# Where a weight tile is split around three norms in a two-layer diffusion trunk: ahead of the modulation instead of behind it

## What is computed

```python
def rmsnorm(x, g):
    y = xf * lax.rsqrt(jnp.mean(xf * xf, axis=-1, keepdims=True) + EPS)
    return (y * g.astype(jnp.float32)).astype(x.dtype)
def modulate(x, shift, scale):
    return x * (1 + scale) + shift
...
for layer in range(DEPTH):
    hp = modulate(rmsnorm(xp, norm1_g[layer]), p_sh1, p_sc1)
    hs = modulate(rmsnorm(xs, norm1_g[layer]), s_sh1, s_sc1)
    # layer 0: Hyena convolution and mLSTM; layer 1: windowed attention -> yp, ys
    xp = xp + p_g1 * yp
    xs = xs + s_g1 * ys
    hp = modulate(rmsnorm(xp, norm2_g[layer]), p_sh2, p_sc2)
    hs = modulate(rmsnorm(xs, norm2_g[layer]), s_sh2, s_sc2)
    # layer 0: dense SwiGLU (1024 -> 2816 -> 1024); layer 1: two of eight expert SwiGLUs
    xp = xp + p_g2 * fp
    xs = xs + s_g2 * fs
```

## Time and profile before

| what | value |
|---|---|
| three runs | 1495.99, 1496.56, 1505.28 us; median 1496.56 |
| profiled execution | 1495.99 us |
| its span in the trace | 1494.2 us, 16385 instructions |
| PE busy | 1365.6 us, 91% |
| DVE busy | 1044.5 us, 70% |
| ACT busy | 818.6 us, 55% |
| weight splits, ACT L494 (raw and arena) | 326 casts, 1.90 us each |
| weight splits, DVE L501 (raw and arena) | 326 subtractions, 2.28 us each |
| mean granted clock of PE | 0.955 of full |

### The profile page before, as it was taken

The page is one execution under the profiler, slowest core; times in us unless marked ns, Lnnn a source line. Parts: engine busy times, 40 slices in busy tenths (PEclk is TensorE's granted clock), DMA queues, the critical chain, the costliest instruction groups (busy, mean ns, idle before and its releaser), DMA issues.

```text
span 1494.2 us, 16385 instructions
## 1 busy us (share of the span) xinstructions
PE 1365.6 (91%) x6400; PEld 1067.1 (71%) x6400; DVE 1044.5 (70%) x1015; ACT 818.6 (55%) x908; POOL 25.4 (2%) x44
## 2 busy tenths in 40 slices
PE   5888898589999987788999999999999999999994
PEld 1555463268888766777888888888888888888783
DVE  0473336455554476556889889898898998988985
ACT  1433121144334455445777777777777777777772
POOL 3000000000000020000000000000000000000000
PEclk9899998699999999888999999999999999999997
DMA  9888677255566540244999999999999999999990
GB/s 330 285 284 307 232 252 264 90 167 170 172 194 188 179 129 32 86 169 141 339 365 351 356 334 353 365 357 352 332 347 364 364 350 341 347 349 369 351 348 30
DMA packets 288116, 400.94 MB, mean 268 GB/s; under 512 B 15973, under 2 KB 224064, under 8 KB 287968
## 3 DMA queue, kind: packets, MB, share of 16 engines
q1 hardware_dynamic: 282048, 391.23, 77.2%
q0 software_dynamic: 1792, 4.28, 1.0%
q10 hardware_dynamic: 4192, 4.31, 0.8%
HBM read 397.93 MB, written 1.84 MB: 268 GB/s over the span
## 4 chain that ended last, share of the span: by engine, by line
PE 79%; DVE 4%; ACT 2%; DMA 1%; issue 1%; SPq 0%; DVEq 0%; ACTq 0%
PE bank L1740 76%; PE bank L2097 2%; DMA raw<-in_w_ada 1%; PE bank L1791 1%; ACT arena L1027 1%; PE bank L2196 0%; ACT arena L1037 0%; SPq L602 0%; DVE arena L1730 0%; DVE xn L1179 0%; DVE arena L1504 0%; DVE x L1505 0%; DVE x L1731 0%; DVE Gb L1198 0%; ACT Gb L796 0%
## 5 line engine op out<-in xcount | busy, mean ns | idle before, releaser
L501 DVE TENSOR_TENSOR w_lo<-raw,w_hi 128x2048 fp32r<-128x2048 f32 (+1 forms) x238 | 543.3, 2283 | 154.4 <-ACT w_hi L494 153.1
L494 ACT CAST w_hi<-raw 128x2048 fp32r<-128x2048 f32 (+1 forms) x238 | 451.8, 1898 | 165.4 <-PE bank L1740 94.2
L1740 PE MATMUL bank<-w_hi,x_hi 128*128 128x512 f32 x1072 | 436.2, 407 | 23.1 <-issue 15.3
L1740 PE MATMUL bank<-w_lo,x_hi 128*128 128x512 f32 x1072 | 424.9, 396 | 0.0
L1740 PE MATMUL bank<-w_hi,x_lo 128*128 128x512 f32 x1072 | 422.4, 394 | 0.0
L1740 PEld LDWEIGHTS bank<-w_hi,x_hi 128*128 128x128 f32 x1072 | 203.5, 190 | 71.6 <-issue 26.3
L1740 PEld LDWEIGHTS bank<-w_hi,x_lo 128*128 128x128 f32 x1072 | 203.7, 190 | 47.0
L1740 PEld LDWEIGHTS bank<-w_lo,x_hi 128*128 128x128 f32 x1072 | 204.1, 190 | 39.2 <-issue 0.2
L501 DVE TENSOR_TENSOR w_lo<-arena,w_hi 128x2048 fp32r<-128x2048 f32 x88 | 201.7, 2292 | 36.9 <-ACT w_hi L494 36.9
L494 ACT CAST w_hi<-arena 128x2048 fp32r<-128x2048 f32 x88 | 168.0, 1909 | 27.8 <-PE bank L1740 27.8
L1740 PE MATMUL bank<-w_hi,g_hi 128*128 128x512 f32 x440 | 174.0, 395 | 1.8 <-DVE g_lo L1461 1.8
(11 more groups left out here) (285 smaller groups left out, 940.6 us busy)
## 6 DMA issues: line engine op xcount, KB each, us to landing
raw<-in_moe_w SPq DMA_DIRECT2D x352, 512.0 KB, 5.4
arena<-in_moe_w SPq DMA_DIRECT2D x176, 512.0 KB, 5.4
raw<-in_w_ada SPq DMA_DIRECT2D x96, 512.0 KB, 6.7
raw<-in_ff_w SPq DMA_DIRECT2D x66, 512.0 KB, 4.5
raw<-in_ev_w_in SPq DMA_DIRECT2D x28, 512.0 KB, 6.8
raw<-in_at_w_qkv SPq DMA_DIRECT2D x12, 512.0 KB, 4.6
raw<-in_ev_w_out SPq DMA_DIRECT2D x8, 512.0 KB, 7.7
raw<-in_at_w_out SPq DMA_DIRECT2D x8, 512.0 KB, 4.6
```

Source lines behind the costliest of these rows:

```text
L494: nc.scalar.copy(w_hi[:, t % SPL, c], place[:, c]).then_inc(hi_ok, 1)
L501: nc.vector.tensor_tensor(w_lo[:, t % SPL, c], raw_slot(n)[0][:, c], w_hi[:, t % SPL, c].bitcast(F32), ALU.subtract).then_inc(lo_ok, 1)
L1740: return pe.matmul(out, lhsT, rhs, start=start, stop=stop)
```

## The change

On ACT the three `high` calls of norms 1, 2 and 3 move from behind `take_turned` to in front of it, and so does one `low` call of each seam on DVE. At norm 2 it is the low part of QKV0 + 1 that moves on DVE, while on ACT it is the high part of QKV0 + 2; the low part of QKV0 + 2 stays. No instruction is added or left out, and the streams of PE, SP and POOL stay as they are.

```diff
@@ -967,8 +967,8 @@
             norm_root(1)
+            high(FF0 + 2)
             take_turned(2, 2)
-            high(FF0 + 2)
             for c in range(NCH):
@@ -980,8 +980,8 @@
             eng.wait_ge(stored_st, STATE_STORES)
             norm_root(2)
+            high(QKV0 + 2)
             take_turned(3, 1)
-            high(QKV0 + 2)
             def take_qkv(w):
@@ -1042,8 +1042,8 @@
             eng.wait_ge(stored_kv, 32)
             norm_root(3)
+            high(MOE0 + 2)
             take_turned(5, 3)
-            high(MOE0 + 2)
             warm(ACT.Exp)
@@ -1487,8 +1487,8 @@
             norm_rows(1)
+            low(FF0 + 2)
             take_turned(2, 2)
-            low(FF0 + 2)
             gate_source(1)
@@ -1508,8 +1508,8 @@
             norm_rows(2)
+            low(QKV0 + 1)
             take_turned(3, 1)
-            low(QKV0 + 1)
             low(QKV0 + 2)
@@ -1613,8 +1613,8 @@
             norm_rows(3)
+            low(MOE0 + 2)
             take_turned(5, 3)
-            low(MOE0 + 2)
             L, E = rw[:, 0:16].rearrange("p (g e) -> p g e", g=G), rw[:, 16:32].rearrange("p (g e) -> p g e", g=G)
```

## The result

The changed kernel took 1512.05 us (median of 22 runs, 1501.18 to 1522.61), the kernel before 1497.69 us (22 runs beside them, 1493.90 to 1510.11): ratio 1.0076, 95% interval 1.0056 to 1.0095. That is within 1% of no change, but outside the range I gave (1498.0 to 1506.5). The profiled execution took 1515.6 us (span 1513.8), 19.6 us more span than the profiled one of before. Over all 39 executions recorded of the changed kernel (these 22 among them) the time goes with the mean granted clock: 12 took 1501 to 1507 us at 0.951 to 0.955, 27 took 1510 to 1523 us at 0.941 to 0.947.

The account below looks back on a forecast made before the run. The prediction took PE to bound the kernel, with time to win or lose only at the three norm seams. Later starts of 4.0 us plus 2.35 of clock made 6.3 us, so 1502.6 us, range 1498.0 to 1506.5.

Parts of the forecast that it names:

- The starts: At the three norm seams, PE's next work starts later by 2.0, 0.3 and 1.7 us, 4.0 us in all.
- DVE's order decides: First seam: DVE's modulation waits for the moved subtraction, so PE's first wide matmul starts 1.99 us later.
- POOL beside the subtraction: Second seam: POOL's memset adds 0 to the moved DVE subtraction; upper bound 0.9 us.
- The clock at the first seam: Behind the first seam: one half-speed stretch of PE follows the longer gap, +1.65 us, bounds 0 to 3.3.
- The clock at the router: Third seam: all the router's first matmuls run at the half level, +0.7 us, bounds 0 and 0.9.
- the stretch from there to the end of the experts otherwise of the same length: Sign to check: after the first seam's half level, no other change in length through the experts, attention included.
- B: Rival: first and second seams each get a second half-speed stretch, 9.6 us in all, 1505.9 us; chance 0.13.
- C: Rival: not slower; second seam's restart and router both run at the full level, giving back 3.95 us, 1496.3; chance 0.05.
- A: Rival: later starts alone, first seam again escapes the half level, +4.0 us, about 1500.3; chance 0.22.

Follow-up runs that it names:

- highs-only run: Kernel before with only ScalarE's three high splits moved ahead of the turned rows, VectorE's low splits left behind them: 1499.50 us, ratio 1.0015.
- run with pauses: Kernel before with no split moved; VectorE does idle work on a free buffer where the change has its splits: 1511.76 us, ratio 1.0082.
- norm 3 alone: Kernel before with both splits of norm 3 only moved, as in the change: 1501.34 us, ratio 1.0014.
- norm 1 alone: Kernel before with both splits of norm 1 only moved, as in the change: 1500.24 us, ratio 1.0008.
- norm 2 alone: Kernel before with both splits of norm 2 only moved, as in the change: 1501.02 us, ratio 1.0014.
- attention filled: Kernel before with matmuls of constants filling PE's gaps in the attention stage only, no split moved: 1494.94 us, ratio 0.9976.

## Why the prediction missed

**The starts: right.** +1.77, +0.20 and +1.50 for a forecast of 2.0, 0.3 and 1.7. The argument that DVE's order decides held: the highs-only run and the run with pauses show it from both sides. The estimate was 0.2 too high at norms 1 and 3 because the cast starts 0.20 us after the root's own start (I had put it 0.32 and 0.31 behind it), and the subtraction 0.04 and 0.03 after the cast's end (I had 0.10).

**POOL beside the subtraction: right.** It took 2.27 us beside a memset that was at work from 535.88, no more than the 2.29 elsewhere. The rule of the Trainium skill ("SBUF — State Buffer", section "SBUF: two separate sides"), that a VectorE operation with two SBUF inputs competes only with a GpSimd operation that reads SBUF, agrees with that.

**The clock at the first seam: the number by luck.** Against the profile of before the FFN lost 1.56 us (forecast 1.65). But the term took from one profile that the kernel before has no half level behind the first seam, and three of the five profiles with that seam as before have it. From norm 1's transposes to the second scores the kernels with late starts at norms 1 and 2 took 263.1 to 263.2 us without a further delay; with VectorE's order at norm 1 as before two profiles took 259.6 and 259.7 and three 262.5. So the delay of 2 us and the clock together cost 3.5 us or 0.6, by the execution that one compares with.

**The clock at the router: too low.** The router cost 0.83 us, for a forecast of 0.7 (whose own terms, 10 x 0.08, make 0.8). What follows it was priced at nothing and took 1.35 more, with half-speed matmuls at 697 to 702 us. How this divides is not steady: with norm 3 as before the experts too took 1.0 to 1.3 us more in three profiles, and seam and router less. The whole is steady. From norm 3's transposes to the end of the span it took 835.4 to 835.8 us in six profiles with VectorE's order at norm 3 as before and no seam filled, and 838.9 to 839.4 in six with a later start there. That is some 3.5 us, where 2.4 was forecast.

**The step that failed** is "the stretch from there to the end of the experts otherwise of the same length", that is, a term of 0 for attention and its out-projection. It measured +9.40 us in the profiled execution, and filling PE's gaps in attention brought the two kernels' medians from 14.4 us apart to 5.9. I had looked for clock losses only at the three places where the gap itself changes. I had not asked what a stage further on, with gaps of its own, does when it starts a little earlier or later. The rows for it were there: attention of the kernel before ran at a mean clock of 0.82 with PE busy for 35.03 of 45.15 us, so the level was already falling and rising inside it, and a stage like that has a loss that can grow and shrink. An estimate of its bounds could have been had from them as well: 35.03 us at 0.82 are 28.7 us of work at the full level, 6.3 less, and 57 at the half level, 12 more than the whole 45.15. The same product of the changed kernel (40.45 at 0.71) is 28.7 too. The runs later gave 41.15 for the stretch at the full level (4 us less) and 52.3 in the worst profile (7 more). With such bounds in the range the time would have been inside it.

Of the rivals, B (twice the clock, 1505.9) was nearest by size, but its mechanism, a second half-speed stretch behind seams 1 and 2, is not what happened: the FFN lost 1.56, as forecast, and QKV 0.02. C's thought that the level's changes may fall otherwise against the work was right in kind and I used it only for a gain. A and the forecast are not far from a part of the executions: 12 of the 39 took 1501 to 1507 us. None of those was profiled, so the runs do not show that attention lost nothing in them.

The Trainium skill ("TensorE: Matmul & The Clock Gate", section "Why this matters for your kernels") warns of idle gaps between bursts. Filling the gaps bears it out: with attention and the seams filled, the granted clock was 1.00 over all of attention. Part 1 of the same page ("What's actually happening") puts the penalty of the ramp below 1% of a typical kernel's span. Filling gave 0.68% in the kernel before and 0.85% in the changed one (1.0076 to 0.9990). This is not the whole price of the half level here, since the filled kernels still ran at a mean granted clock of 0.963 and 0.965. And already that part is as much as the whole effect that was to be forecast, so it can't be left out of a sum for a small change.

**What stays open.** The runs do not say what fixes the moments at which the level changes. The work alone does not: the profiles of before and of norm 3 alone differ in it ahead of norm 3, where the programs are the same. What they show is which side of the two each kernel is on (the table of the second scores), and that delays at norms 1 and 2 together took it to the other side in all five profiles that have them, while norm 1 alone and norm 2 alone did not, in one profile each. Why a late start of 1.45 us more gave back 5 us there, and one of 2.9 us nothing, I can't say; with one profile of each, it may be chance of the execution. And the medians (14.4 us apart) and the profiled executions (19.6) differ. Of that, 3.07 us lie ahead of norm 1; the rest I can't divide, since I have profiles of one execution of each kernel only.

## What to carry to other kernels

Price a delay at the place where it happens and then ask of every later stage in which TensorE works in short bursts what it does when it starts a microsecond off: its granted clock in the profile before (0.82 in this attention) tells that it can lose or win, and an estimate of its length at the full level and at the half level gives the bounds. Before a clock term is priced from one profile, take a second one of the same kernel: here the same FFN took 196.5 or 198.1 us. Work that may go behind a norm is better there, if it would stand in VectorE's chain. Where PE must wait, matmuls of constants into a free bank gave 9.7 us here (1498.00 to 1488.30), while no order of the splits measured here was faster than the kernel before.

## What the runs showed of the hardware that I had not expected

- Idle work on VectorE at three places (3.19 us at norms 1 and 3, 2.13 at norm 2, 8.5 in all) slowed the program by 13.6 us (1511.76 against 1498.17).
- With 1.45 us more of delay at norm 2, attention and its out-projection took 5.4 us less in the profiled execution (75.94 instead of 81.35), and the median was no higher.
- One and the same feed-forward stage, behind the same code, took 196.5 us in two profiles (before, norm 2 alone) and 198.1 in two others (norm 3 alone, attention filled), with the half level behind the seam in the latter.
- The half level held for 20 us (631 to 651) in which PE was busy for 16.76.
- The attention stage was shorter where its first matmuls ran slow: in five profiles the second scores took 4.57 us, PE waited 1.22 us, and the stage with its out-projection 68.5 to 72.0; in five they took 2.94 us, PE waited 2.85 us, and the stage took 74.6 to 81.5. That the one is the cause of the other is not shown.
- Attention and its out-projection took 68.0 to 68.4 us in the four kernels with filled gaps, between 68.5 and 81.5 in the ten without.
